# A chunked RWKV-7 recurrence inside a fused encoder trunk: triangular inverses from 8x8 blocks and four doubling levels in place of 4x4 blocks and five

## The chip, the cores and the metric

One core of one Trainium2 chip runs the whole program in one launch. The metric is the device time of one execution in microseconds. The kernel before takes 1693.85 us, the median of three runs (1692.18 to 1694.16).

## The reference, cut to what matters

The input is 256 tokens of 2048 channels, float32. Two layers follow each other. Each layer normalises x, multiplies it by one wide input matrix, and feeds three branches: a stick-breaking attention, a latent attention, and the RWKV-7 recurrence. The three gated results are projected, merged, projected once more and added to x. The change touches only the recurrence:

```python
def rwkv7_scan(r, decay, k, v, a_vec, b_vec):
    def step(state, inp):
        r_t, w_t, k_t, v_t, a_t, b_t = inp
        sa = jnp.einsum('bhij,bhj->bhi', state, a_t)
        state = (state * w_t[:, :, None, :] + sa[..., None] * b_t[:, :, None, :]
                 + v_t[..., None] * k_t[:, :, None, :])
        return state, jnp.einsum('bhij,bhj->bhi', state, r_t)
```

There are 8 heads of 64 channels. The kernel does not step through the tokens. It takes 128 tokens at a time, which turns the recurrence into matrix products and the inverse of one 128x128 unit triangular matrix for each head and each half of the sequence.

## The kernel before, in words

**The dense stream.** Most of the time goes to matrix products with weights read from memory. The weights come in chunks of two blocks of 128 rows by (mostly) 512 columns; there are 280 chunks in a layer. SyncE fetches a chunk into a ring of four slots. ScalarE copies it, rounded, into `w_hi` (the function `split` of the scalar program, line 1034), and VectorE subtracts to get the remainder `w_lo` (`split` of the vector program, line 1400). TensorE then runs 12 matmuls of 512 columns for the chunk (`dense_to`, line 730): two row blocks, two halves of the sequence, and three products of high and low parts. Before each chunk it waits for that chunk's `w_lo`. ScalarE and VectorE stay up to `LEAD` = 3 chunks ahead, and the four slots of `w_hi` and `w_lo` let them go no further.

**The order of the other work.** Everything else is cut into steps and laid between the chunks in an order written out by hand. `STEPS` (line 161) is a list of weights, one for each step; `beat_at` (line 165) spreads the steps over chunk positions 50 to 208 of each layer in proportion to the weights. Each engine's program calls `beat()` at the end of a step, and that issues its dense work up to the position. TensorE can stop at half a chunk; ScalarE and VectorE round the position down to a whole chunk. When VectorE's program has passed position n, it has issued the remainders of the chunks up to number n + 2 (counted from 0).

**The recurrence.** `rw_pair(p)` handles two heads, so it is run four times in a layer and eight times in all. The four matrices of a pair (two heads, two halves) are worked side by side. TensorE forms them (`rw_pe` count 2, lines 808 to 814), and VectorE copies them under a mask into `AM` (line 1529). Then:

- GpSimd gathers the 32x32 blocks on the diagonal of the four matrices into the compact tile `UC` (line 573).
- VectorE inverts the 4x4 blocks inside them. It picks three diagonals out of `UC` by a multiplication with a mask and a sum (lines 1539 and 1540), transposes them (1541), solves for the three diagonals of the inverse by six short operations (1544 to 1549), transposes back (1550), and spreads the diagonals over the columns again (1552 to 1554) into `WC`, `WT` and `WA`. One `beat()` lies between line 1550 and line 1552. These operations hang on each other, and `link` puts a semaphore wait on VectorE behind nearly every one. I call the part up to line 1550 the first part, and the rest the second part.
- Doubling levels follow on TensorE (line 816). A level is a group G1 of four small matmuls, a ScalarE copy of its result, a group G2 of four small matmuls, and an addition and transposes on VectorE. Levels 1 to 3 go from 4x4 to 32x32, level 4 to 64x64 and level 5 to 128x128.

The position of TensorE at which the pairs of a layer form their matrices is 50.5, 73.5, 92.5 and 111.5. From there it issues dense work for the next four steps and then begins level 1, at 55.5, 78.5, 97.5 and 116.5.

Of the kernel before, what the change touches and what calls it, by code (L numbers as in the profile page):

```python
# [32 lines left out]
ALU = mybir.AluOpType  # L33
ACT = mybir.ActivationFunctionType
X = mybir.AxisListType.X

DEPTH, SEQ, DM = 2, 256, 2048
P = 128
# [16 lines left out]
C_GATE = C_RG + RWW  # L55
DECAY = float(np.exp(-0.5))
MID = P // 2 - 1
LEVELS = 5
LEVELS_IN = 4
KC = 2  # L60
RING = 4
HALF_RING = 4
# [7 lines left out]


K_ID, K_INC, K_NTRI, K_NONE, K_RWM, K_LEV = 0, 128, 256, 384, 512, 1024
K_COS = K_LEV + 128 + 64 * LEVELS_IN
K_SIN = K_COS + 64
K_COL = K_SIN + 64
K_END = K_COL + 2
# [2 lines left out]
def constants():  # L79

    c = np.zeros((P, K_END), np.float32)
    i = np.arange(P)
    row, col = i[:, None], i[None, :]
    c[:, K_ID:K_ID + P] = row == col
    past_mid = (row <= MID).astype(np.float32)
    c[:, K_INC:K_INC + P] = -DECAY * ((row <= col).astype(np.float32) - past_mid)
    c[:, K_NTRI:K_NTRI + P] = -(row >= col).astype(np.float32)
    c[:, K_NONE:K_NONE + P] = -1.0
    strict, incl = (row < col), (row <= col)
    c[:, K_RWM:K_RWM + 512] = np.concatenate([strict, incl, strict, incl], 1)  # L90
    for q in range(4):
        r = slice(32 * q, 32 * q + 32)
        for k in range(4):
            at = K_LEV + 32 * k
            c[r, at:at + 32] = ((col == row + (k + 1) % 4) & (row // 4 == col // 4))[r, r]
        for n in range(LEVELS_IN):
            b = 2 ** (n + 1)
            joined = (row // (2 * b) == col // (2 * b)) & (row // b < col // b) | (n == 0)
            at = K_LEV + 128 + 64 * n + 32 * (q % 2)
            c[r, at:at + 32] = joined[r, r]  # L100
    half = ROPE // 2
    freqs = (np.float32(10000.0) ** (-np.arange(half, dtype=np.float32) / np.float32(half))).astype(np.float32)
    ang = np.arange(SEQ, dtype=np.float32)[:, None] * freqs[None, :]
    for h in range(HALVES):
        c[:, K_COS + h * half:K_COS + (h + 1) * half] = np.cos(ang[h * P:(h + 1) * P])
        c[:, K_SIN + h * half:K_SIN + (h + 1) * half] = np.sin(ang[h * P:(h + 1) * P])
    c[:, K_COL] = -DECAY * (i > MID)
    c[:, K_COL + 1] = -DECAY * (i <= MID)

    return c  # L110
# [39 lines left out]
AT_KK = AT_Z + 1  # L150
AT_DECAY = AT_KK + 9
AT_PAIRS = AT_DECAY + 5
RW_STEPS = [1, 1.2, 1, 1.5, 1.8] + [0.88, 0.98] * LEVELS + [0.85] * 6
LATENT_STEPS = [2, 2.5]
GN_STEPS = [0.9] * 8
ML_PREP, ML_VISITS = [1.1, 1.2, 1.3, 1.2, 1.4, 1.4], [2, 1.5, 1.4]
# [33 lines left out]
AT_RW, AT_ML1, AT_SB = END["mg1"] + 2, END["mg1"] + 4, END["br0"]  # L190


RW_PE, RW_ACT, RW_DVE, RW_POOL = 8 + 2 * LEVELS, 5 + LEVELS, 5 + 2 * LEVELS, 9


def program(nc, x, norm_g, w_in, mla_q_norm_g, mla_kv_norm_g, mla_w_uq, mla_w_ukv, mla_qn_g, mla_kn_g,
# [3 lines left out]
    with ExitStack() as ctx:  # L200
# [13 lines left out]
        con = sb("con", [P, K_END])  # L214
# [15 lines left out]
        def take(n):  # L230
            a = arena[:, used[0]:used[0] + n]
            used[0] += n
            assert used[0] <= ARENA, used[0]
            return a
# [4 lines left out]
        def units(n, u):  # L239
            return take(n).rearrange("p (u c) -> p u c", u=u)  # L240
# [10 lines left out]
        PV = halved(3072)  # L251
# [10 lines left out]
        UC, WC = units(128, 4), units(128, 4)  # L262
# [14 lines left out]
        WF = units(512, 4)  # L277
        WT, WT6, XB = units(256, 4), units(256, 4), units(256, 4)
        (WAE, WA), (LME, LM), (LM5E, LM5), (X5E, X5), (X6E, X6) = (edged() for _ in range(5))
        DIAG, DIAG_T, INVERSE = units(96, 3), units(96, 3), units(128, 4)  # L280
        ZEROS = arena[:, at_tb:used[0]]
        WIDE = take(512).rearrange("p (k u c) -> p k u c", k=4, u=4)
        QKM, PP = again(at_tb, lambda: units(1536, 12), lambda: units(768, 2))
        PT, = again(at_tt, lambda: units(768, 2))
        sb_tiles = [again(at_tb, *[lambda n=n: take(n) for n in (512, 384, 384)])]
# [37 lines left out]
        eps, eps_gn, bias_kk = cells(1), cells(1), cells(1)  # L323

        ident = con[:, K_ID:K_ID + P]
        diagonals = con[:, K_LEV:K_LEV + 128].rearrange("p (k c) -> p k c", k=4)
        level = [con[:, K_LEV + 128 + 64 * n:K_LEV + 192 + 64 * n] for n in range(LEVELS_IN)]
        ntri, none = con[:, K_NTRI:K_NTRI + P], con[:, K_NONE:K_NONE + P]
        cosx = con[:, K_COS:K_COS + 64].rearrange("p (h c) -> p h c", h=2)
        sinx = con[:, K_SIN:K_SIN + 64].rearrange("p (h c) -> p h c", h=2)  # L330
# [17 lines left out]
        preset = sem("preset")  # L348
# [157 lines left out]
        def _(pool):  # L506
# [7 lines left out]
            for l in range(DEPTH):  # L514
# [26 lines left out]
                nc.gpsimd.tensor_copy(AM[:, :, 0:P], ident.unsqueeze(1).to_broadcast([P, 4, P])).then_inc(preset[l], 1)  # L541
                nc.gpsimd.memset(ZEROS, 0.0).then_inc(preset[l], 1)
                pool.wait_ge(preset[l], 8)
                nc.gpsimd.memset(INVERSE[:, 3, :], 1.0).then_inc(preset[l], 1)
                gate, beats = [0], [0]

                def dense_to(end):
# [18 lines left out]
                for p in range(4):  # L566
# [4 lines left out]
                    for q in range(4):  # L571
                        r = slice(32 * q, 32 * q + 32)
# [4 lines left out]
                    for a in range(2):  # L577
                        r = slice(64 * a, 64 * a + 32)
# [8 lines left out]
                    if p < 3:  # L587
# [3 lines left out]
                        for d in range(4):  # L591
                            for i in range(4):
                                j = (i + d) % 4
# [25 lines left out]
                for p in range(4):  # L619
# [3 lines left out]
                    for d in range(4):  # L623
                        for i in range(4):
                            j = (i + d) % 4
# [46 lines left out]
                for n in range(12):  # L672
# [5 lines left out]
                    if 6 <= n < 10:  # L678
                        j = n - 6
# [3 lines left out]
                        c = slice(j * 512, (j + 1) * 512)  # L683
# [5 lines left out]
                    if n >= 5 and n % 3 == 2:  # L689
                        j = n // 3 - 1  # L690
# [696 lines left out]
        def _(dve):  # L1387
            v = nc.vector
            at, group, beats, order = [0], [GI["rg"]], [0], [0]

            def link(ins):

                order[0] += 1
                ins.then_inc(dve_seq, 1)
                dve.wait_ge(dve_seq, order[0])

            def tt(o, a, b, op):
                return v.tensor_tensor(o, a, b, op)  # L1398
# [117 lines left out]
            def rw_pair(p):  # L1516
                e = RW_PE * p
                c = slice(p * P, (p + 1) * P)
# [11 lines left out]
                last.then_inc(rw_dve, 1)  # L1530
                beat(2)
                dve.wait_ge(rw_pool, 4 * RW_POOL * l + RW_POOL * p + 4)
                def over_columns(t, n):
                    return t[:, 0:n, 0:4].unsqueeze(3).to_broadcast([P, n, 4, 32])

                def over_units(n):
                    return diagonals[:, 0:n, :].unsqueeze(2).to_broadcast([P, n, 4, 32])

                link(tt(WIDE[:, 0:3], UC.unsqueeze(1).to_broadcast([P, 3, 4, 32]), over_units(3), ALU.mult))
                link(v.tensor_reduce(DIAG[:, :, 0:4], WIDE[:, 0:3], axis=X, op=ALU.add))  # L1540
                link(v.transpose(DIAG_T, DIAG))
                d1, d2, d3 = (DIAG_T[:, k, :] for k in range(3))
                t1, t2 = WIDE[:, 3, 0, :], WIDE[:, 3, 1, :]
                tt(t1[:, 0:31], d1[:, 0:31], d1[:, 1:32], ALU.mult)
                link(tt(t2[:, 0:30], d2[:, 0:30], d1[:, 2:32], ALU.mult))
                tt(d2[:, 0:31], d2[:, 0:31], t1[:, 0:31], ALU.add)
                link(tt(d3[:, 0:30], d3[:, 0:30], t2[:, 0:30], ALU.add))
                link(tt(t1[:, 0:31], d1[:, 0:31], d2[:, 1:32], ALU.mult))
                link(tt(d3[:, 0:31], d3[:, 0:31], t1[:, 0:31], ALU.add))
                link(v.transpose(INVERSE[:, 0:3, :], DIAG_T))  # L1550
                beat()
                link(tt(WIDE, over_columns(INVERSE, 4), over_units(4), ALU.mult))
                link(tt(WIDE[:, 0:2], WIDE[:, 0:2], WIDE[:, 2:4], ALU.add))
                link(tt(WC, WIDE[:, 0], WIDE[:, 1], ALU.add))
                for g in range(2):
                    last = v.transpose(WT[64 * g:64 * g + 64, :, 32 * g:32 * g + 32], WC[64 * g:64 * g + 64, :, :])
                last.then_inc(rw_dve, 1)
# [4 lines left out]
                for n in range(1, LEVELS_IN):  # L1562
                    beat()
                    dve.wait_ge(rw_pe, 4 * RW_PE * l + e + 2 * n + 2)
                    for g in range(2):
                        half = slice(32 * g, 32 * g + 32)
                        t = WT[64 * g:64 * g + 64, :, half]
                        last = tt(t, t, G2[0:64, :, half], ALU.add)
                    last.then_inc(rw_dve, 1)
                    dve.wait_ge(rw_dve, 4 * RW_DVE * l + RW_DVE * p + 2 * n + 3)  # L1570
                    for q in (1, 3) if n == LEVELS_IN - 1 else range(4):
                        r = slice(32 * q, 32 * q + 32)
                        last = v.transpose(WA[r, :, q % 2 * 32:q % 2 * 32 + 32], WT[r, :, q // 2 * 32:q // 2 * 32 + 32])
                    last.then_inc(rw_dve, 1)
                    if p < 3:
                        if n == 1 and p:
                            dve.wait_ge(ops_moved, 3 * l + p)
                        for i in range(n - 1, n + (n == 3)):
                            s = (KK, R[:, :, 0:512], AA, R[:, :, 512:1024])[i]
                            last = v.transpose(OPS_TURN[:, :, i * P:(i + 1) * P], s[:, :, (p + 1) * P:(p + 2) * P])  # L1580
                        if n == 3:
                            last.then_inc(ops_turned, 1)
                    if n == LEVELS_IN - 1:
                        for q in range(4):
                            r = slice(32 * q, 32 * q + 32)
                            v.transpose(WF[r, :, r], WT[r, :, q // 2 * 32:q // 2 * 32 + 32])
                    beat()
# [156 lines left out]
            for l in range(DEPTH):  # L1744
# [26 lines left out]
                for i in range(3):  # L1771
# [3 lines left out]
                    c = slice(i * 512, (i + 1) * 512)  # L1775
# [113 lines left out]
                for j in range(4):  # L1889
                    dense_to(merged_at(j))  # L1890
                    for s in range(2):
                        dve.wait_ge(mt_act[l], 2 * j + s + 1)
                        k = slice(4 * j + 2 * s, 4 * j + 2 * s + 2)
# [31 lines left out]
```

## Time and profile before

| what | value |
|---|---|
| median of three runs | 1693.85 us |
| the profiled execution, first to last instruction (its span) | 1690.5 us |
| TensorE matmul busy | 1677.6 us (99%) |
| TensorE weight load busy | 1399.2 us (83%) |
| VectorE busy | 1134.9 us (67%) |
| ScalarE busy | 836.6 us (49%) |
| GpSimd busy | 487.8 us (29%) |
| bytes moved by DMA | 332.82 MB, mean 197 GB/s |
| granted TensorE clock | full speed in every slice |

The profiled execution has only its span as its own time; the timed runs also hold what lies ahead of the first and behind the last instruction, and their median is 3.35 us above that span. The page of the profile gives busy time by engine, the slices of the span, the chain of work that ended last, and the costliest groups of instructions. One caution applies to TensorE: matmuls overlap in its pipeline, so one that is listed with 0.39 us is followed by the next one 0.23 us after it began.

### The profile page before, as it was taken

To read this page: it belongs to the slowest core of one execution; us is meant where nothing else is said; L and a number is where in the kernel's file an instruction comes from. 1 tells how busy PE (TensorE), PEld (TensorE's weight loads), DVE (VectorE), ACT (ScalarE), POOL (GpSimd) and SP (SyncE) were. 2 spreads that over 40 slices of the span, in tenths; PEclk is the share of its full clock that TensorE was granted. 3 is DMA by queue.
4 is the path that set the end of the run, shared out by engine and by line. 5 is a ranking of instruction groups with operands and counts; after the bars stand their busy time and mean duration, and the time that the engine had idled before them with its cause. 6 is when DMAs were issued, how large, how long until landed. Compare 5 with 4: busy or idle time off the path is not lost.

```text
span 1690.5 us, 22088 instructions
## 1 busy us (share of the span) xinstructions
PE 1677.6 (99%) x8394; PEld 1399.2 (83%) x8394; DVE 1134.9 (67%) x1579; ACT 836.6 (49%) x1181; POOL 487.8 (29%) x722
## 2 busy tenths in 40 slices
PE   8999999999999999999999999999999999999999
PEld 7878888888888888888888788888888888888887
DVE  5668575766976566886656775756669666578853
ACT  6454453435544455554454454434445554555532
POOL 1011212410343426362410112233203534244500
PEclk9999999999999999999999999999999999999999
DMA  8865655655666557785687555556556565668754
GB/s 277 243 193 182 175 177 170 184 165 173 178 184 176 173 164 234 236 302 188 205 269 226 176 186 172 187 152 188 174 167 178 167 178 177 192 212 279 267 193 157
DMA packets 176913, 332.82 MB, mean 197 GB/s; under 512 B 19516, under 2 KB 32746, under 8 KB 176808
## 3 DMA queue, kind: packets, MB, share of 16 engines
q1 hardware_dynamic: 167048, 297.86, 57.7%
q0 software_dynamic: 9584, 33.48, 5.7%
q8 instruction: 66, 1.08, 0.3%
q14 instruction: 39, 0.32, 0.1%
q10 hardware_dynamic: 176, 0.07, 0.0%
HBM read 311.20 MB, written 16.78 MB: 194 GB/s over the span
## 4 chain that ended last, share of the span: by engine, by line
PE 92%; DVE 3%; ACT 2%; DMA 2%; issue 1%; SPq 1%; ACTq 0%; DVEq 0%
PE D L707 83%; PE B L707 8%; DMA ring<-in_w_in 2%; DVE w_lo L1398 1%; ACT w_hi L1026 1%; DVE xy L1398 0%; ACT arena L1026 0%; ACT gev L1026 0%; PE B L898 0%; DVE arena L1398 0%; DVE gev L1444 0%; PE B L877 0%; SPq L435 0%; ACT L1026 0%; DVE arena L1428 0%
## 5 line engine op out<-in xcount | busy, mean ns | idle before, releaser
L1398 DVE TENSOR_TENSOR w_lo<-ring,w_hi 128x1024 fp32r<-128x1024 f32 (+3 forms) x560 | 675.7, 1219 | 342.1 <-ACT w_hi L1026 334.0
L1026 ACT ACTIVATE w_hi<-ring 128x1024 fp32r<-128x1024 f32 (+3 forms) x560 | 575.0, 1038 | 463.9 <-PE D L707 361.5
L707 PE MATMUL D<-w_hi,ht_hi 128*128 128x512 f32 (+2 forms) x1728 | 681.3, 394 | 3.0 <-DVE w_lo L1398 2.8
L707 PE MATMUL D<-w_hi,ht_lo 128*128 128x512 f32 (+2 forms) x1728 | 666.0, 385 | 0.0
L707 PE MATMUL D<-w_lo,ht_hi 128*128 128x512 f32 (+2 forms) x1728 | 665.1, 385 | 0.0
L707 PEld LDWEIGHTS D<-w_hi,ht_hi 128*128 128x128 f32 x1728 | 325.1, 188 | 71.4 <-issue 7.8
L707 PEld LDWEIGHTS D<-w_hi,ht_lo 128*128 128x128 f32 x1728 | 324.5, 188 | 65.3
L707 PEld LDWEIGHTS D<-w_lo,ht_hi 128*128 128x128 f32 x1728 | 325.2, 188 | 59.0 <-issue 0.5
L609 POOL COPY arena<-arena 32x256 f32<-32x256 f32 x240 | 163.1, 680 | 144.7 <-DVE arena L1428 109.3
L707 PEld LDWEIGHTS B<-arena 128*66 128x66 f32 (+3 forms) x1312 | 134.2, 165 | 24.3 <-issue 8.2
L707 PE MATMUL B<-arena 128*66 128x64 f32 (+7 forms) x1312 | 144.7, 263 | 0.6 <-ACT arena L1026 0.6
L1026 ACT ACTIVATE arena<-B 64x128 f32<-64x128 f32 (+5 forms) x146 | 50.2, 350 | 189.2 <-PE B L707 183.9
L626 POOL COPY arena<-arena 32x384 f32<-32x384 f32 x128 | 95.7, 748 | 136.0 <-PE B L707 103.8
L707 PE MATMUL D<-w_hi,mt_lo 128*128 128x512 f32 x256 | 100.7, 393 | 0.0
L707 PE MATMUL D<-w_lo,mt_hi 128*128 128x512 f32 x256 | 100.4, 392 | 0.0
L707 PE MATMUL D<-w_hi,mt_hi 128*128 128x512 f32 x256 | 99.7, 389 | 0.0
L552 POOL DMA_DIRECT2D gate_spill<-gev x24 | 17.8, 742 | 246.9 <-ACT gev L1026 245.8
L1398 DVE TENSOR_TENSOR arena<-arena 128x1024 f32<-128x1024 f32 (+5 forms) x136 | 75.0, 561 | 5.1 <-DMA arena<-arena 1.6
L573 POOL COPY arena<-arena 32x128 f32<-32x128 f32 x32 | 24.4, 764 | 171.6 <-DVE arena L1529 170.2
L1026 ACT ACTIVATE arena<-arena 128x1024 f32<-128x1024 f32 (+5 forms) x88 | 59.0, 670 | 15.2 <-DVE arena L1398 11.6
L1026 ACT ACTIVATE gev<-D,small 128x512 f32<-128x512 f32 (+1 forms) x64 | 40.5, 681 | 45.0 <-PE D L707 44.8
L707 PEld LDWEIGHTS D<-w_lo,mt_hi 128*128 128x128 f32 x256 | 48.1, 188 | 11.0
(160 smaller groups left out, 1376.9 us busy)
## 6 DMA issues: line engine op xcount, KB each, us to landing
ring<-in_w_in SPq DMA_DIRECT2D x368, 512.0 KB, 4.5
ring<-in_w_out SPq DMA_DIRECT2D x64, 512.0 KB, 5.2
ring<-in_w_br_mla SPq DMA_DIRECT2D x32, 512.0 KB, 5.2
gate_spill<-gev POOLq DMA_DIRECT2D x24, 512.0 KB, 4.7
arena<-gate_spill POOLq DMA_DIRECT2D x24, 512.0 KB, 5.2
ring<-in_mla_w_ukv SPq DMA_DIRECT2D x16, 512.0 KB, 4.0
ring<-in_w_br_rw SPq DMA_DIRECT2D x16, 512.0 KB, 5.2
ring<-in_w_br_sb SPq DMA_DIRECT2D x16, 512.0 KB, 5.2
```

The lines of the kernel that those rows point to most:

```text
L552: pool.dma_start(spill[n].rearrange("(h p) c -> p h c", p=P), gev[:, n % 2, :, :]).then_inc(spilled[n % 2][l], 16)
L573: nc.gpsimd.tensor_copy(UC[r, :, :], AM[r, :, r]).then_inc(rw_pool, 1)
L609: nc.gpsimd.tensor_copy(moved[32 * j:32 * j + 32, :, :, i, :], turned[32 * i:32 * i + 32, :, :, j, :]).then_inc(quadrants[l], 1)
L626: nc.gpsimd.tensor_copy(moved[32 * j:32 * j + 32, :, i, :], turned[32 * i:32 * i + 32, :, j, :]).then_inc(ml_quarters, 1)
L707: return nc.tensor.matmul(o, a, b, start=start, stop=stop, skip_group_check=True)
L1026: return nc.scalar.activation(o, i, fn, **kw)
L1398: return v.tensor_tensor(o, a, b, op)
```

## The change

A block is now 8x8 (`EDGE`), so one doubling level goes: `LEVELS` 4 for 5, `LEVELS_IN` 3 for 4. VectorE picks seven diagonals instead of three. First it folds each row's own 8x8 block out of the 32 columns of `UC` into eight columns, `INNER`; the diagonals are taken from there. The seven diagonals of the inverse are solved by six rounds of two operations. The solution is spread over 8 columns (`SOLVED`) and then over 32. Scratch tiles move into `PV`, and the constants hold other masks. The weights of a pair's steps change, with the same sum of 20.9 as before. With them the same helper `beat_at` puts TensorE's level 1 at positions 57, 80, 99 and 117.5. GpSimd runs one level mask fewer. The operands of the next pair are turned two at a time in levels 1 and 2, not one, one and two in levels 1 to 3.

```diff
-LEVELS = 5
-LEVELS_IN = 4
+LEVELS = 4
+LEVELS_IN = 3
+EDGE = 8
...
-RW_STEPS = [1, 1.2, 1, 1.5, 1.8] + [0.88, 0.98] * LEVELS + [0.85] * 6
+RW_STEPS = [1, 1.2, 1, 1.7, 2.96] + [0.92, 1.02] * LEVELS + [0.88] * 6
...
-                link(tt(WIDE[:, 0:3], UC.unsqueeze(1).to_broadcast([P, 3, 4, 32]), over_units(3), ALU.mult))
-                link(v.tensor_reduce(DIAG[:, :, 0:4], WIDE[:, 0:3], axis=X, op=ALU.add))
+                blocks = own_block.unsqueeze(1).unsqueeze(3).to_broadcast([P, 4, 32 // EDGE, EDGE])
+                wide = WIDE[:, 0:128].rearrange("p (u j c) -> p u j c", u=4, j=32 // EDGE)
+                link(tt(wide, UC.rearrange("p u (j c) -> p u j c", c=EDGE), blocks, ALU.mult))
+                link(v.tensor_reduce(INNER, wide.rearrange("p u j c -> p u c j"), axis=X, op=ALU.add))
+                wide = WIDE[:, 0:32 * (EDGE - 1)].rearrange("p (k u c) -> p k u c", k=EDGE - 1, u=4)
+                link(tt(wide, INNER.unsqueeze(1).to_broadcast([P, EDGE - 1, 4, EDGE]),
+                        diagonals[:, 0:EDGE - 1, :].unsqueeze(2).to_broadcast([P, EDGE - 1, 4, EDGE]), ALU.mult))
+                link(v.tensor_reduce(DIAG[:, :, 0:4], wide, axis=X, op=ALU.add))
                 link(v.transpose(DIAG_T, DIAG))
-                d1, d2, d3 = (DIAG_T[:, k, :] for k in range(3))
-                t1, t2 = WIDE[:, 3, 0, :], WIDE[:, 3, 1, :]
-                tt(t1[:, 0:31], d1[:, 0:31], d1[:, 1:32], ALU.mult)
-                link(tt(t2[:, 0:30], d2[:, 0:30], d1[:, 2:32], ALU.mult))
-                tt(d2[:, 0:31], d2[:, 0:31], t1[:, 0:31], ALU.add)
-                link(tt(d3[:, 0:30], d3[:, 0:30], t2[:, 0:30], ALU.add))
-                link(tt(t1[:, 0:31], d1[:, 0:31], d2[:, 1:32], ALU.mult))
-                link(tt(d3[:, 0:31], d3[:, 0:31], t1[:, 0:31], ALU.add))
-                link(v.transpose(INVERSE[:, 0:3, :], DIAG_T))
+                link(v.tensor_copy(INVERSE_T, DIAG_T))
+                for m in range(1, EDGE - 1):
+                    n, c0 = EDGE - 1 - m, 32 - m
+                    link(tt(TERMS[:, 0:n, 0:c0], DIAG_T[:, 0:n, m:32],
+                            INVERSE_T[:, m - 1:m, 0:c0].to_broadcast([P, n, c0]), ALU.mult))
+                    solved = INVERSE_T[:, m:EDGE - 1, 0:c0]
+                    link(tt(solved, solved, TERMS[:, 0:n, 0:c0], ALU.add))
+                link(v.transpose(INVERSE[:, 0:EDGE - 1, :], INVERSE_T))
                 beat()
-                link(tt(WIDE, over_columns(INVERSE, 4), over_units(4), ALU.mult))
-                link(tt(WIDE[:, 0:2], WIDE[:, 0:2], WIDE[:, 2:4], ALU.add))
-                link(tt(WC, WIDE[:, 0], WIDE[:, 1], ALU.add))
+                wide = WIDE.rearrange("p (u c k) -> p u c k", u=4, c=EDGE)
+                link(tt(wide, INVERSE[:, :, 0:4].rearrange("p k u -> p u k").unsqueeze(2)
+                        .to_broadcast([P, 4, EDGE, EDGE]), diagonals.rearrange("p k c -> p c k").unsqueeze(1)
+                        .to_broadcast([P, 4, EDGE, EDGE]), ALU.mult))
+                link(v.tensor_reduce(SOLVED, wide, axis=X, op=ALU.add))
+                link(tt(WC.rearrange("p u (j c) -> p u j c", c=EDGE),
+                        SOLVED.unsqueeze(2).to_broadcast([P, 4, 32 // EDGE, EDGE]), blocks, ALU.mult))
...
-                        for i in range(n - 1, n + (n == 3)):
+                        for i in (2 * n - 2, 2 * n - 1):
```

## Rows read from the trace of the kernel before

**Rows 1.** The page: busy time by engine, and shares of the chain that ended last.
```profile
PE 1677.6 (99%) x8394; PEld 1399.2 (83%) x8394; DVE 1134.9 (67%) x1579; ACT 836.6 (49%) x1181; POOL 487.8 (29%) x722
PE 92%; DVE 3%; ACT 2%; DMA 2%; issue 1%; SPq 1%; ACTq 0%; DVEq 0%
```

**Rows 2.** Waits, whole span: waiter, releaser, us in total, times, longest.
```profile
PE D L707 <- DVE w_lo L1398: 2.8, 9, 0.5
```

**Rows 3.** Timeline of TensorE, third pair, layer 0: start, length, instruction.
```profile
293.16 0.50 PE L707 MATMUL D<-w_hi,ht_hi 128*128 128x512 f32 x1
...
297.19 0.39 PE L707 MATMUL D<-w_hi,ht_lo 128*128 128x512 f32 x1
...
299.91 0.39 PE L707 MATMUL D<-w_hi,ht_lo 128*128 128x512 f32 x1
...
305.57 0.39 PE L707 MATMUL D<-w_hi,ht_hi 128*128 128x512 f32 x1
...
306.94 0.64 PE L707 MATMUL B<-arena 128*66 128x64 f32 x8
...
310.24 0.64 PE L707 MATMUL B<-arena 128*66 128x64 f32 x8
```

**Rows 4.** Timeline of VectorE, GpSimd and ScalarE, same pair.
```profile
293.28 2.62 DVE L1529 COPY_PREDICATED arena<-con,B 128x512 f32<-128x512 uint32 x4 [3.25 <-PE B L707]
...
295.77 2.46 DVE L1398 TENSOR_TENSOR w_lo<-ring,w_hi 128x1024 fp32r<-128x1024 f32 x2
295.97 3.10 POOL L573 COPY arena<-arena 32x128 f32<-32x128 f32 x4 [18.72 <-DVE arena L1529]
...
299.11 0.56 DVE L1398 TENSOR_TENSOR arena<-arena,con 128x384 f32<-128x384 f32 x1 [0.88 <-POOL arena L573]
...
300.60 1.18 DVE L1398 TENSOR_TENSOR arena<-arena 128x31 f32<-128x31 f32 x6
...
302.12 2.36 DVE L1398 TENSOR_TENSOR w_lo<-ring,w_hi 128x1024 fp32r<-128x1024 f32 x2
303.06 1.27 ACT L1026 ACTIVATE gev<-D,small 128x512 f32<-128x512 f32 x2 [1.60 <-PE D L707]
...
307.61 0.56 ACT L1026 ACTIVATE arena<-B 64x128 f32<-64x128 f32 x2 [2.34 <-PE B L707]
```

**Rows 5.** Timeline of VectorE, first pair of layer 0.
```profile
152.33 2.64 DVE L1529 COPY_PREDICATED arena<-con,B 128x512 f32<-128x512 uint32 x4 [2.38 <-PE B L707]
...
158.41 0.56 DVE L1398 TENSOR_TENSOR arena<-arena,con 128x384 f32<-128x384 f32 x1 [1.22 <-POOL arena L573]
```

**Rows 6.** VectorE groups by line and shape: count, busy us, mean ns, idle before.
```profile
L1398 DVE TENSOR_TENSOR arena<-arena,con 128x128 f32<-128x128 f32 x48 | 12.0, 291 | 0.5
L1580 DVE STREAM_TRANSPOSE xy<-arena 128x256 f32<-128x256 f32 x18 | 7.3, 431 | 0.4
L1398 DVE TENSOR_TENSOR arena<-arena 128x31 f32<-128x31 f32 x32 | 6.2, 194 | 1.1
L1398 DVE TENSOR_TENSOR arena<-arena 128x256 f32<-128x256 f32 x14 | 6.0, 425 | 0.4
L1540 DVE TENSOR_REDUCE arena<-arena 128x12 f32<-128x384 f32 x8 | 4.4, 553 | 0.3
L1541 DVE STREAM_TRANSPOSE arena<-arena 128x96 f32<-128x96 f32 x8 | 2.2, 279 | 0.3
L1816 DVE COPY arena<-arena 128x128 f32<-128x128 f32 x2 | 0.5, 227 | 0.1
```

**Rows 7.** Timeline: TensorE waits for a `w_lo` that is late.
```profile
1296.58 1.21 DVE L1398 TENSOR_TENSOR w_lo<-ring,w_hi 128x1024 fp32r<-128x1024 f32 x1
...
1297.03 0.39 PE L707 MATMUL D<-w_hi,ht_lo 128*128 128x512 f32 x1
...
1297.85 0.50 PE L707 MATMUL D<-w_hi,ht_hi 128*128 128x512 f32 x1 [0.43 <-DVE w_lo L1398]
...
1298.18 0.40 PE L707 MATMUL D<-w_lo,ht_hi 128*128 128x512 f32 x1
```

More of the change, by code:

```diff
@@ L72 @@
 K_ID, K_INC, K_NTRI, K_NONE, K_RWM, K_LEV = 0, 128, 256, 384, 512, 1024
-K_COS = K_LEV + 128 + 64 * LEVELS_IN
+K_BLK = K_LEV + EDGE * EDGE
+K_JOIN = K_BLK + 32 // EDGE
+K_COS = K_JOIN + 64 * LEVELS_IN
 K_SIN = K_COS + 64
@@ L92, in constants @@
         r = slice(32 * q, 32 * q + 32)
-        for k in range(4):
-            at = K_LEV + 32 * k
-            c[r, at:at + 32] = ((col == row + (k + 1) % 4) & (row // 4 == col // 4))[r, r]
+        for k in range(EDGE):
+            at = K_LEV + EDGE * k
+            c[r, at:at + EDGE] = col[:, 0:EDGE] == row[r] % EDGE + (k + 1) % EDGE
+        c[r, K_BLK:K_BLK + 32 // EDGE] = row[r] % 32 // EDGE == col[:, 0:32 // EDGE]
         for n in range(LEVELS_IN):
-            b = 2 ** (n + 1)
+            b = EDGE // 2 * 2 ** n
             joined = (row // (2 * b) == col // (2 * b)) & (row // b < col // b) | (n == 0)
-            at = K_LEV + 128 + 64 * n + 32 * (q % 2)
+            at = K_JOIN + 64 * n + 32 * (q % 2)
             c[r, at:at + 32] = joined[r, r]
@@ L190 @@
 AT_RW, AT_ML1, AT_SB = END["mg1"] + 2, END["mg1"] + 4, END["br0"]
-RW_PE, RW_ACT, RW_DVE, RW_POOL = 8 + 2 * LEVELS, 5 + LEVELS, 5 + 2 * LEVELS, 9
+RW_PE, RW_ACT, RW_DVE, RW_POOL = 8 + 2 * LEVELS, 5 + LEVELS, 5 + 2 * LEVELS, 5 + LEVELS_IN
 def program(nc, x, norm_g, w_in, mla_q_norm_g, mla_kv_norm_g, mla_w_uq, mla_w_ukv, mla_qn_g, mla_kn_g,
@@ L279, in program @@
         (WAE, WA), (LME, LM), (LM5E, LM5), (X5E, X5), (X6E, X6) = (edged() for _ in range(5))
-        DIAG, DIAG_T, INVERSE = units(96, 3), units(96, 3), units(128, 4)
+        DIAG, INVERSE = units(32 * (EDGE - 1), EDGE - 1), units(32 * EDGE, EDGE)
         ZEROS = arena[:, at_tb:used[0]]
-        WIDE = take(512).rearrange("p (k u c) -> p k u c", k=4, u=4)
+        DIAG_T = units(32 * (EDGE - 1), EDGE - 1)
+        spare = [PV[:, 0, 256 * n:256 * n + 256] for n in range(4)]
+        WIDE = spare[0]
+        INVERSE_T = spare[1][:, 0:32 * (EDGE - 1)].rearrange("p (k c) -> p k c", k=EDGE - 1)
+        TERMS = spare[2].rearrange("p (k c) -> p k c", k=EDGE)
+        INNER, SOLVED = (spare[3][:, 32 * n:32 * n + 32].rearrange("p (u c) -> p u c", u=4) for n in range(2))
         QKM, PP = again(at_tb, lambda: units(1536, 12), lambda: units(768, 2))
@@ L325, in program @@
         ident = con[:, K_ID:K_ID + P]
-        diagonals = con[:, K_LEV:K_LEV + 128].rearrange("p (k c) -> p k c", k=4)
-        level = [con[:, K_LEV + 128 + 64 * n:K_LEV + 192 + 64 * n] for n in range(LEVELS_IN)]
+        diagonals = con[:, K_LEV:K_BLK].rearrange("p (k c) -> p k c", k=EDGE)
+        own_block = con[:, K_BLK:K_JOIN]
+        level = [con[:, K_JOIN + 64 * n:K_JOIN + 64 * n + 64] for n in range(LEVELS_IN)]
         ntri, none = con[:, K_NTRI:K_NTRI + P], con[:, K_NONE:K_NONE + P]
@@ L543, in _ @@
                 pool.wait_ge(preset[l], 8)
-                nc.gpsimd.memset(INVERSE[:, 3, :], 1.0).then_inc(preset[l], 1)
+                nc.gpsimd.memset(INVERSE[:, EDGE - 1, :], 1.0).then_inc(preset[l], 1)
                 gate, beats = [0], [0]
@@ L1532, in rw_pair @@
                 dve.wait_ge(rw_pool, 4 * RW_POOL * l + RW_POOL * p + 4)
[L1533 to L1537, printed above, removed]
-                link(tt(WIDE[:, 0:3], UC.unsqueeze(1).to_broadcast([P, 3, 4, 32]), over_units(3), ALU.mult))
-                link(v.tensor_reduce(DIAG[:, :, 0:4], WIDE[:, 0:3], axis=X, op=ALU.add))
@@ L1577, in rw_pair @@
                             dve.wait_ge(ops_moved, 3 * l + p)
-                        for i in range(n - 1, n + (n == 3)):
+                        for i in (2 * n - 2, 2 * n - 1):
                             s = (KK, R[:, :, 0:512], AA, R[:, :, 512:1024])[i]
                             last = v.transpose(OPS_TURN[:, :, i * P:(i + 1) * P], s[:, :, (p + 1) * P:(p + 2) * P])
-                        if n == 3:
+                        if n == LEVELS_IN - 1:
                             last.then_inc(ops_turned, 1)
```

## The prediction, made before the changed kernel was run

> **What bounds the kernel now.** I read the page first. TensorE is busy for 1677.6 of 1690.5 us, and 92% of the chain that ended last is TensorE's own work [rows 1]. Next I read the waits: TensorE stood waiting for a late `w_lo` for only 2.8 us in the whole span, in nine places [rows 2]. So an instruction taken from TensorE is worth its time, VectorE's time is worth nothing as long as the remainders come early enough, and a change that makes them late costs TensorE directly. Last I read the timelines of one pair of heads on TensorE [rows 3] and on the other engines [rows 4], because the change moves both of these.
>
> **What TensorE saves.** A level is two groups of four small matmuls. The two groups in rows 3 begin 3.30 us apart (306.94 to 310.24), and between them lie the first group and 12 dense matmuls. Twelve dense matmuls with nothing between take 2.72 us (297.19 to 299.91). So a group costs 0.58 us. Two groups in each of eight pairs are 16 groups, and 16 x 0.58 = 9.3 us saved. What goes with the level on VectorE (two additions, four transposes), ScalarE (two copies) and GpSimd (one mask) lies beside TensorE's work and brings nothing by itself.
>
> **What VectorE's first part takes now.** Before, it runs from 299.11 to 302.12, 3.0 us [rows 4]. The gap behind a linked operation is 0.03 us: from 300.60 to 302.12 lie 1.18 us of short operations and a transpose of 0.28 us [rows 4, 6], which leaves 0.06 us for two gaps. The new first part has 19 linked operations, priced along the rows of [rows 6] by elements per partition:
> - the multiplication with the block mask, 128 elements: 0.29 + 0.03 = 0.32 us;
> - the sum over it: the row for 384 elements is 0.55 us, the same as a multiplication of that size, so again 0.32 us;
> - the multiplication and the sum for seven diagonals, 224 elements, between 0.291 and 0.425 us: 0.39 + 0.03 = 0.42 us each;
> - two transposes of 224 elements, between 0.279 us (96) and 0.431 us (256): 0.43 us each with the gap;
> - the copy of 224 elements; the row for 128 elements is 0.227 us, and I take 0.30 us with the gap;
> - twelve operations in six rounds over 186, 150, 116, 84, 54 and 26 elements. Between 0.194 us (31), 0.291 us (128) and 0.425 us (256) these come to 0.352, 0.314, 0.279, 0.247, 0.217 and 0.189 us. With six gaps that is 1.78 us, and there are two operations in a round: 3.56 us.
>
> The sum is 0.64 + 0.84 + 0.86 + 0.30 + 3.56 = 6.20 us, against 3.0 us before.
>
> Its bounds: if short operations cost nearly nothing per element (0.19 us each for the twelve), the part takes 5.3 us. If rows of 26 to 31 elements, or reading every eighth element, run at half the rate per element, it takes 7.1 us (616 elements twice and 128 once, 1.05 ns each, with something off because not all is hit). Rows 6 show broadcasts at the full rate and no such stride, so I take 6.2.
>
> The Trainium skill's page "Vector Engine (DVE) Microarchitecture Reference", section "Measured stream behaviour on trn2", speaks against the change here: a port that steps over elements one by one loses up to about 1.5 ns on each. By it the sum into `INNER` (128 elements, stride eight) would take some 0.2 us more, and all eight pairs 1.5 us more. No row here shows such a stride.
>
> **What of it TensorE feels.** Before the first part VectorE issues the remainders up to position 52 in the first pair (94 in the third, and so on), which is two of them at 295.77 in [rows 4]. They cover TensorE to position 55.0 (97.0). TensorE restarts at 50.5 (92.5), so it meets the first missing `w_lo` after 4.5 chunks, 54 matmuls. In [rows 3] that is 293.16 to 305.57, 12.41 us. The new weights of the steps move level 1 back, but they do not put a remainder inside or ahead of the first part.
>
> The first part can begin only when GpSimd's four copies are done, 3.10 us in [rows 4]. It began 5.83 us after the masked copy in the third pair [rows 4] and 6.08 us after it in the first [rows 5]; the other six pairs lie between, and the mean of the eight is 5.95 us. The masked copy begins 0.12 us after TensorE's restart (293.28 to 293.16), so the part begins 6.07 us after the restart. Then come 6.20 us of first part and 1.21 us for the remainder behind it [rows 7]: 13.48 us. This is 1.07 us after TensorE wants it. In the kernel before the same sum is 6.07 + 3.0 + 1.2 = 10.3 us, 2.1 us early, and that reserve is what hides the part today.
>
> The handing over costs something too. In [rows 7] the late subtraction ends at 1297.79, the matmul begins at 1297.85, and the next one begins 0.33 us later instead of 0.23: 0.06 + 0.10 = 0.16 us. So TensorE loses 1.23 us in each pair, and eight pairs make 9.8 us.
>
> **What else moves.**
> - Second part, behind the remainder and one more: 256 elements twice, 128 once, two transposes and the mask of `WA` come to some 2.3 us, and then a third remainder. It ends 4.6 us after TensorE's late restart, and TensorE wants it after two chunks, 5.4 us. It is hidden with 0.8 us to spare. If both new operations ran at half rate (+0.5 us) it still would be.
> - G2 of level 1 stands half a chunk behind G1 in three of four pairs, where it was a whole chunk. ScalarE's copy between them takes 0.56 us and starts 0.67 us after G1, at 307.61 in [rows 4], 1.23 us against 1.9 us of TensorE's work. In the second pair G1 is at position 80, which is also the end of a gate group, and ScalarE's two evictions of it (1.27 us, as at 303.06 in rows 4) come ahead of the copy. That makes 2.2 us against 1.9: 0.3 us in each layer, 0.5 us with rounding. Bounds: nothing, and 1.3 us a layer.
> - The turned operands of the next pair come 0.4 of a step earlier, and GpSimd's 16 copies of them start no later than before. The lesser mask on GpSimd lies beside this. Both nothing.
> - VectorE has 1.1 us more in a pair (3.2 more in the first part, 0.3 less in the second, 1.8 less for the level). It idles a third of the span, so only the place matters, which is priced above.
>
> **The sum.** -9.3 + 9.8 + 0.5 = +1.0 us on the span of 1690.5 us. The runs shown have a median 3.35 us above the span, and nothing of the change touches that part. So 1693.85 + 1.0 = 1694.9 us. The measurement can tell about 0.2%, 3.4 us, from no change.
>
> **The rivals.**
> - *The first part stays hidden, and the saving is the result.* If the part takes 5.1 us or less (1.1 us under my sum), TensorE never waits and the time is 1693.85 - 9.3 + 0.5 = 1685 us. For it: the reserve of 2.1 us is real, and only a third of the extra 3.2 us has to go. Against it: the 19 operations would have to cost less than the flat price of 0.19 us for the twelve short ones. In between, every tenth of a microsecond off the part is worth 0.8 us. The result counts as faster when the part takes under 5.65 us.
> - *VectorE's part is longer than the sizes say (the other sign).* The place is the same remainder behind the first part; the mechanism is a slower rate of strided or short-rowed operands, or a wait by each of the 19 links that is longer than 0.03 us. At 6.8 us for the part, the wait is 1.83 us in each pair: 14.6 - 9.3 + 0.5 = +5.8 us, 1699.7 us. It decides from 6.5 us on, where the total passes +3.4 us. For it: all 19 operations hang on each other. Against it: the linked operations in the rows show only the 0.03 us.
> - *The remainders are late twice*, behind the second part too. It needs the second part to be 0.8 us longer than 2.3 us. Then some tenths of a microsecond are added in each pair, +1 to +4 us, at most 1699. I count it with the case before.
>
> **How the numbers follow.** The forecast case (the part between 5.65 and 6.5 us, a wait of 0.7 to 1.5 us in each pair) gets 0.46. The hidden or half hidden part, faster by over 0.2%, gets 0.22. The slower cases get 0.32. The range goes down to a part of 5.4 us (-6.4 from the forecast, 1688.5) and up to one of just under 7.0 us (+6.1, 1701.0). It leaves out the wholly hidden case and the worst lateness, together some 2 in 10.
>
> **What would show it.** Right: 64 fewer small matmuls (128 records fewer on TensorE); a row "PE D waits for DVE w_lo" of about 10 us, one wait of 1.1 to 1.3 us in each of eight pairs, each at the first chunk behind the first part; the first part 6.2 us long in the timeline of VectorE. Wrong: eight pairs without such a wait and a span of 1681 to 1682 us; a first part under 5.6 or over 6.6 us; TensorE waiting at the small groups of level 1 for `WT` or for ScalarE's copy more than for the remainders; or a wait at the chunk behind the second part.

## The result and the profile after

The changed kernel takes 1694.0 us, the median of 21 runs (1693.21 to 1695.92). The kernel before, run beside it, takes 1692.02 us in 21 runs. The ratio is 1.0012, with a 95% interval of 1.0007 to 1.0018. So the change makes the kernel slower by 2.0 us, clear of noise but within the 0.2% that the prediction called no change. The forecast was +1.0 us. The forecast of the time itself, 1694.9 us, lies closer than that, and this is luck: it was built on the median of three runs, 1693.85 us, which is 1.8 us above the median of 21. The span went from 1690.5 to 1692.1 us.

The page of the changed kernel, the rows that answer to [rows 1] and [rows 2] (engines, the chain, and the wait of TensorE for a late remainder: total, times, longest):

```profile
PE 1671.4 (99%) x8266; PEld 1392.0 (82%) x8266; DVE 1142.6 (68%) x1603; ACT 831.9 (49%) x1165; POOL 477.7 (28%) x714
...
PE 90%; DVE 6%; POOL 1%; DMA 1%; ACT 1%; issue 1%; SPq 0%; ACTq 0%; DVEq 0%
```

```profile
PE D L717 <- DVE w_lo L1408: 11.0, 12, 1.4
```

TensorE has 128 instructions fewer (8394 to 8266), which are the 64 small matmuls at two records each, and 6.2 us less work. In exchange it now waits 11.0 us for `w_lo`, not 2.8. The chain has 6% of VectorE in it where it had 3%, and 1% of GpSimd, which had none. These are the masked copy, GpSimd's gathering and the first part, which now lie ahead of the remainder for which TensorE waits.

Eight of those twelve waits are the pairs'. The timeline of TensorE in the changed kernel, only the instructions that waited, one for each pair:

```profile
166.48 0.50 PE L717 MATMUL D<-w_hi,ht_hi 128*128 128x512 f32 x1 [1.38 <-DVE w_lo L1408]
...
243.56 0.50 PE L717 MATMUL D<-w_hi,ht_hi 128*128 128x512 f32 x1 [1.04 <-DVE w_lo L1408]
...
372.79 0.50 PE L717 MATMUL D<-w_hi,ht_hi 128*128 128x512 f32 x1 [1.27 <-DVE w_lo L1408]
...
1004.09 0.50 PE L717 MATMUL D<-w_hi,ht_hi 128*128 128x512 f32 x1 [1.11 <-DVE w_lo L1408]
...
1081.17 0.50 PE L717 MATMUL D<-w_hi,ht_hi 128*128 128x512 f32 x1 [1.04 <-DVE w_lo L1408]
...
1145.77 0.50 PE L717 MATMUL D<-w_hi,ht_hi 128*128 128x512 f32 x1 [1.05 <-DVE w_lo L1408]
...
1210.46 0.50 PE L717 MATMUL D<-w_hi,ht_hi 128*128 128x512 f32 x1 [1.28 <-DVE w_lo L1408]
```

With the third pair (1.03, below) they add up to 9.20 us. The third pair of layer 0 in full, first TensorE (it answers to [rows 3]), from its restart to level 1:

```profile
294.53 0.50 PE L717 MATMUL D<-w_hi,ht_hi 128*128 128x512 f32 x1
...
306.72 0.39 PE L717 MATMUL D<-w_hi,ht_lo 128*128 128x512 f32 x1
308.14 0.50 PE L717 MATMUL D<-w_hi,ht_hi 128*128 128x512 f32 x1 [1.03 <-DVE w_lo L1408]
308.48 0.39 PE L717 MATMUL D<-w_lo,ht_hi 128*128 128x512 f32 x1
...
313.72 0.64 PE L717 MATMUL B<-arena 128*66 128x64 f32 x8
315.64 0.64 PE L717 MATMUL B<-arena 128*66 128x64 f32 x8
```

And VectorE in the same pair (it answers to [rows 4]). The part of lines 1546 to 1559 with the multiplications between them is the first part:

```profile
300.46 0.29 DVE L1408 TENSOR_TENSOR arena<-arena,con 128x128 f32<-128x128 f32 x1 [0.88 <-POOL arena L583]
300.78 0.39 DVE L1546 TENSOR_REDUCE arena<-arena 128x32 f32<-128x128 f32 x1
301.20 0.39 DVE L1408 TENSOR_TENSOR arena<-arena,con 128x224 f32<-128x224 f32 x1
301.63 0.39 DVE L1550 TENSOR_REDUCE arena<-arena 128x28 f32<-128x224 f32 x1
302.05 0.41 DVE L1551 STREAM_TRANSPOSE arena<-arena 128x224 f32<-128x224 f32 x1
302.50 0.28 DVE L1552 COPY arena<-arena 128x224 f32<-128x224 f32 x1
302.81 3.57 DVE L1408 TENSOR_TENSOR arena<-arena 128x186 f32<-128x186 f32 x12
306.42 0.41 DVE L1559 STREAM_TRANSPOSE arena<-arena 128x224 f32<-128x224 f32 x1
306.86 2.36 DVE L1408 TENSOR_TENSOR w_lo<-ring,w_hi 128x1024 fp32r<-128x1024 f32 x2
309.14 0.66 DVE L1408 TENSOR_TENSOR arena<-arena,con 128x256 f32<-128x256 f32 x1
...
311.28 0.43 DVE L1408 TENSOR_TENSOR arena<-arena,con 128x256 f32<-128x256 f32 x1
```

Read the two side by side. VectorE waits 0.88 us for GpSimd, begins the first part at 300.46 and ends it at 306.86, 6.40 us later. Only then does it begin the remainder that TensorE wants. TensorE issued its last matmul at 306.72, would have issued the next at 306.95, and issues it at 308.14.

From the restart to level 1 TensorE takes 19.19 us for 78 dense matmuls. In [rows 3] 60 matmuls took 13.78 us, and 18 more at 2.72 us a dozen are 4.08 us, together 17.86. So a pair loses 1.33 us, which is 0.3 us more than the idle time in the row. That column counts from the modelled end of the last matmul, and it does not hold the slow restart.

### The profile page after: what moved, and what is told of

Its sections match the earlier page's. It is cut to its first block, busy times and chain, and to the rows that moved or that the text cites. A ratio compares the mean times of both kernels' runs of the same rounds, so it can differ in the third digit from the quotient of the medians.

```text
span 1692.1 us, 21816 instructions
## 1 busy us (share of the span) xinstructions
PE 1671.4 (99%) x8266; PEld 1392.0 (82%) x8266; DVE 1142.6 (68%) x1603; ACT 831.9 (49%) x1165; POOL 477.7 (28%) x714
## 4 chain that ended last, share of the span: by engine, by line
PE 90%; DVE 6%; POOL 1%; DMA 1%; ACT 1%; issue 1%; SPq 0%; ACTq 0%; DVEq 0%
PE D L717 81%; PE B L717 8%; DVE arena L1408 2%; POOL arena L583 1%; DVE arena L1539 1%; DVE w_lo L1408 1%; DMA ring<-in_w_in 1%; ACT w_hi L1036 0%; DMA xy<-in_x 0%; PE B L908 0%; ACT arena L1036 0%; PE B L790 0%; PE B L887 0%; DVE arena L1559 0%; DVE arena L1551 0%
## 5 line engine op out<-in xcount | busy, mean ns | idle before, releaser
L717 PEld LDWEIGHTS B<-arena 128*66 128x66 f32 (+3 forms) x1184 | 124.2, 168 | 20.9 <-issue 7.7
L717 PE MATMUL B<-arena 128*66 128x64 f32 (+7 forms) x1184 | 134.4, 268 | 0.0
L1036 ACT ACTIVATE arena<-B 64x128 f32<-64x128 f32 (+5 forms) x130 | 45.7, 359 | 172.3 <-PE B L717 167.0
L1408 DVE TENSOR_TENSOR arena<-arena 128x1024 f32<-128x1024 f32 (+9 forms) x168 | 86.4, 515 | 5.1
L717 PEld LDWEIGHTS D<-w_hi,mt_lo 128*128 128x128 f32 x256 | 48.0, 188 | 11.2
```

The lines of the kernel that those rows point to most:

```text
L717: return nc.tensor.matmul(o, a, b, start=start, stop=stop, skip_group_check=True)
L1036: return nc.scalar.activation(o, i, fn, **kw)
```

## The experiments

Eight kernels were run. Ratios are to the kernel before in the same rounds: its median was 1691.67 us beside the first four kernels, 1692.18 beside the next three and 1692.36 beside the last.

### The remainder moved ahead of the first part

```diff
-RW_STEPS = [1, 1.2, 1, 1.7, 2.96] + ...
+RW_STEPS = [1, 1.2, 1.9, 1.5, 2.26] + ...
```

> The changed kernel with only the weights of a pair's steps altered (same sum): VectorE issues one more remainder before the first part, in the 0.9 to 1.2 us in which it stood idle for GpSimd's copies. TensorE's positions, its instructions and the first part stay as they are. Theory (a remainder comes late behind the first part because of its place, about 1.2 us in each pair): the eight waits go, TensorE's wait for w_lo falls from 11.0 us to about 2.5 us, and the time from 1694.0 to about 1684.5 us, ratio to the kernel before 0.995 to 0.996. Rival (VectorE's or the chain's total length is what costs, wherever it lies): the time stays near 1694 us, ratio 1.001. Rival (the waits only move to another place, level 1 or the next remainder): 1690 to 1694 us and waits of the same sum at another position.

Measured: 1684.35 us against 1691.67, ratio 0.9955 (0.9941 to 0.9969). VectorE's timeline in the third pair shows what moved. The single remainder at 298.16 is new there, and the first part begins behind it:

```profile
295.16 2.44 DVE L1408 TENSOR_TENSOR w_lo<-ring,w_hi 128x1024 fp32r<-128x1024 f32 x2
298.16 1.23 DVE L1408 TENSOR_TENSOR w_lo<-ring,w_hi 128x1024 fp32r<-128x1024 f32 x1 [0.56 <-ACT w_hi L1036]
299.57 0.29 DVE L1408 TENSOR_TENSOR arena<-arena,con 128x128 f32<-128x128 f32 x1 [0.19 <-POOL arena L583]
...
306.00 1.23 DVE L1408 TENSOR_TENSOR w_lo<-ring,w_hi 128x1024 fp32r<-128x1024 f32 x1
```

The new remainder lies where VectorE had stood idle for GpSimd, but it does not fit in there. VectorE first waits 0.56 us for ScalarE's copy and then 0.19 us for GpSimd, so it idles 0.75 us where it idled 0.88. The first part begins 7.02 us behind TensorE's restart at 292.55, and in the changed kernel it was 5.93 (294.53 to 300.46). GpSimd is held up too, its four copies in the changed kernel and in this one:

```profile
297.32 3.10 POOL L583 COPY arena<-arena 32x128 f32<-32x128 f32 x4 [18.26 <-DVE arena L1539]
```

```profile
295.34 4.20 POOL L583 COPY arena<-arena 32x128 f32<-32x128 f32 x4 [18.25 <-DVE arena L1539]
```

The gain comes from the order. The part begins 1.1 us later, but the first remainder behind it is wanted a whole chunk later, 2.72 us. It is ready at 307.23, and TensorE uses it at 307.68. All eight pairs' waits for `w_lo` are gone. The 4.2 us that are left, in six places, all lie ahead of the first pair of a layer. The first part is as long as before, so its place costs, not its length by itself. The first rival falls. Of the second, that the waits move elsewhere, 0.3 us is true: in the fourth pair of each layer, where level 1 stands six chunks behind the restart and not 6.5, TensorE now arrives before the transposes into `WT` are done:

```profile
372.52 0.69 PE L717 MATMUL B<-arena 128*66 128x64 f32 x8 [0.16 <-DVE arena L1569]
```

This version beats both kernels.

### The first part made longer

```diff
                 link(v.transpose(DIAG_T, DIAG))
+                for _ in range(3):
+                    link(v.transpose(DIAG_T, DIAG))
```

> The changed kernel with its first transpose (224 elements, 0.44 us with the gap) issued three more times in the first part, 1.3 us more there. Theory (no reserve is left, each microsecond of the first part is lost on TensorE in each pair): eight waits of about 2.5 us, 10.5 us more than the changed kernel, 1704.5 us, ratio 1.0075. Rival (the waits have another cause than the length of the first part): within 2 us of the changed kernel.

Measured: 1710.09 us, ratio 1.0109 (1.0096 to 1.0123): 16 us more than the changed kernel, not 10.5. The wait for `w_lo` rose as expected, from 11.0 to 22.4 us, with 2.38 to 2.73 us in each pair. Nearly all of the other 5 us is the granted clock, and the section on the hardware shows it. So the theory held for the wait, and the time missed for a reason that was not in it.

### The first part of the kernel before made longer by 1.2 us and by 3.4 us

```diff
                 link(v.transpose(DIAG_T, DIAG))
+                for _ in range(4):      # 11 in the second kernel
+                    link(v.transpose(DIAG_T, DIAG))
```

> The kernel before with its first transpose (96 elements, 0.31 us with the gap) issued four more times in the first part: 1.24 us more there, no level removed. Theory (a reserve of 2.1 us hides it): no wait is added, the ratio is 1.000 within its interval. Rival (VectorE's time costs in proportion): up to 10 us more, ratio 1.002 to 1.006.

> The kernel before with its first transpose issued eleven more times in the first part: 3.4 us more there, about what the 8x8 blocks add, and no level removed. Theory (3.4 less the reserve of 2.1 leaves 1.3 us late, and 0.16 for the handing over): eight waits of 1.3 to 1.4 us and 11 to 12 us more, 1703.5 us, ratio 1.007. Rival (the waits of the changed kernel come of its other step positions or of its strided operations): no more than 3 us slower, ratio under 1.002.

Measured: 1697.96 us with four, ratio 1.0038 (1.0024 to 1.0052), and 1716.88 us with eleven, ratio 1.0150 (1.0136 to 1.0164). Both are misses: 6 us where I expected none, and 25 where I expected 12. The waits of TensorE show why. With four more, the third pair, and with eleven more, the same pair:

```profile
309.42 0.69 PE L707 MATMUL B<-arena 128*66 128x64 f32 x8 [0.65 <-DVE arena L1558]
```

```profile
312.93 0.50 PE L707 MATMUL D<-w_hi,ht_hi 128*128 128x512 f32 x1 [1.01 <-DVE w_lo L1398]
...
316.11 0.69 PE L707 MATMUL B<-arena 128*66 128x64 f32 x8 [1.51 <-DVE arena L1558]
```

With four, no remainder of a pair is late, so the reserve at the remainders is more than 1.24 us. But the first group of level 1 waits for the transposes into `WT` (line 1558 there, 1556 in the kernel before). The kernel before, VectorE's second part in the third pair:

```profile
305.12 0.76 DVE L1398 TENSOR_TENSOR arena<-arena 128x256 f32<-128x256 f32 x2
305.91 0.63 DVE L1556 STREAM_TRANSPOSE arena<-arena 64x128 f32<-64x128 f32 x2
```

They end at 306.54, and the group begins at 306.94 [rows 3]. The reserve there is 0.4 us, and four transposes of 0.31 us overrun it by 0.84; from the restart to level 1 the third pair takes 14.58 us and not 13.78, 0.80 more. The kernel before has two reserves behind the first part, and the smaller one is at level 1. With eleven more both are overrun: waits of 10.7 us at the remainders and 12.2 us at level 1.

Two rivals are answered here. The time with four more, 1.0038, lies in the range of the rival that VectorE's time costs in proportion, and by itself could not reject it; the place of the waits does, and so does the run with the remainder moved ahead. With eleven more, the first part takes 6.38 us in the third pair of a kernel without the changed positions and operations, and the eight waits at the remainders are 1.00 to 1.35 us, where the changed kernel has 1.03 to 1.38 at 6.40 us. So these waits come from the length of the part, and not from the new positions of the steps or from strides as such.

### Three of the six rounds left out

```diff
-                for m in range(1, EDGE - 1):
+                for m in range(1, 4):
```

> The changed kernel with three of the six rounds of the solution (the diagonals four to seven are not completed, so the inverse is not the reference's). The first part is 1.5 us shorter, the places of the steps are the changed kernel's. Theory (length of the first part against a fixed place): it is 4.9 us instead of 6.4, the eight waits of 1.0 to 1.4 us go, and the time falls by 9 to 11 us to about 1684 us, ratio 0.995, the same as with the remainder moved ahead. Rival (every tenth of a microsecond of VectorE's time counts): the same sign, but then the run with the remainder moved ahead, whose VectorE does all the work, should not have reached 1684 us.

Measured: 1682.27 us, ratio 0.9942 (0.9928 to 0.9956). The wait for `w_lo` is 2.1 us in the whole span; none of the pairs waits. In the third pair the first part runs from 297.41 to 302.32:

```profile
297.41 0.29 DVE L1408 TENSOR_TENSOR arena<-arena,con 128x128 f32<-128x128 f32 x1 [0.88 <-POOL arena L583]
...
299.77 2.07 DVE L1408 TENSOR_TENSOR arena<-arena 128x186 f32<-128x186 f32 x6
301.88 0.41 DVE L1559 STREAM_TRANSPOSE arena<-arena 128x224 f32<-128x224 f32 x1
302.32 2.36 DVE L1408 TENSOR_TENSOR w_lo<-ring,w_hi 128x1024 fp32r<-128x1024 f32 x2
```

A shorter part in the old place and a full part in a better place give the same time within their intervals. This is the rival of the prediction in which the first part stays hidden, met on purpose: a part of 4.9 us, and no wait.

### Level 1 back at its old distance

```diff
-RW_STEPS = [1, 1.2, 1, 1.7, 2.96] + [0.92, 1.02] * LEVELS + [0.88] * 6
+RW_STEPS = [1, 1.2, 1, 1.5, 1.8] + [1.0, 1.1] * LEVELS + [1.0] * 6
```

> The changed kernel with the first five step weights of the kernel before, so that level 1 begins five chunks behind TensorE's restart as before, and not 6.5; the later steps are stretched to keep the sum of 20.9. Theory (there are two reserves: 2.1 us for the remainder, and only 0.3 us at level 1 for WT, of which the run with four more transposes showed the second): the eight waits for w_lo stay at 1.0 to 1.4 us, and eight waits of about 1.5 us at the first group of level 1 come on top, as with eleven more transposes; 13 us more than the changed kernel, about 1707 us, ratio 1.009. Rival (level 1's place does not matter as long as the remainders are the bottleneck): 1694 us.

Measured: 1707.79 us, ratio 1.0092 (1.0078 to 1.0105), as expected. Both kinds of wait, in total, times, longest:

```profile
PE D L717 <- DVE w_lo L1408: 12.5, 16, 1.4
PE B L717 <- DVE arena L1569: 12.1, 8, 1.5
```

Moving level 1 back by one to one and a half chunks is thus worth 14 us in the changed kernel. It opened the smaller reserve, and left the remainder's as it was.

### The TensorE work of one level put back by itself

```diff
-                beat(4)
+                beat(2)
+                pe.wait_ge(rw_dve, 4 * RW_DVE * l + d0 + 2)
+                for _ in range(2):
+                    for u in range(4):
+                        mm(B[3][0:66, 64 * u:64 * u + 64], con[:, 0:66], con[:, 0:64], u == 0, True)
+                    beat()
```

> The kernel with the remainder moved ahead, and with two groups of four matmuls (66 by 64, float32, their result unused) put back between the dense matmuls in each pair: TensorE's work of one level, alone, with nothing waiting for it. Theory (a group costs 0.58 us, 16 groups 9.3 us): 1684.4 + 9.3 = 1693.7 us, ratio to the kernel before 1.001. Rival (the level cost less than reckoned, and the gain of the moved remainder came from somewhere else): 1684 to 1690 us, ratio under 0.9985.

Measured: 1691.65 us, ratio 0.9995 (0.9986 to 1.0004). That is 7.3 us more than the kernel it was built on, where 9.3 was expected. From the two ratios the difference is 0.0040, and their intervals allow it to be between some 4 and 9.5 us. The trace is sharper on the groups. The two groups, with 12 dense matmuls between:

```profile
301.36 0.64 PE L717 MATMUL B<-con 128*66 128x64 f32 x8
...
304.64 0.64 PE L717 MATMUL B<-con 128*66 128x64 f32 x8
```

They begin 3.28 us apart, so a group costs 3.28 - 2.72 = 0.56 us, and sixteen cost 9.0 us. The two profiled executions differ by only 4.5 us (spans of 1684.7 and 1689.2). Of the missing 4.5 us, 2.9 lie outside the pairs, in the waits for late remainders (4.2 and 1.3 us), and 0.3 are the two waits at level 1, which are gone here. The rest, 1.3 us, is not explained.

### The remainder moved ahead in the kernel before

```diff
-RW_STEPS = [1, 1.2, 1, 1.5, 1.8] + ...
+RW_STEPS = [1, 1.2, 1.9, 0.8, 1.6] + ...
```

> The kernel before (4x4 blocks, five levels) with only the weights altered so that one more remainder is issued ahead of the first part, as in the run that reached 1684 us; no other position changes. Theory (the moved remainder is worth something only where a remainder is late, and here none is): 1692 us, ratio 0.9985 to 1.0015. Rival (the gain of that run came from the moved remainder itself and not from the level that went): about 7 us faster, ratio 0.996.

Measured: 1692.49 us against 1692.36, ratio 1.0002 (0.9993 to 1.0011). By itself the move is worth nothing. The 7 us of the first experiment are the level that went, most of it no longer paid back.

## Why the prediction was right, point by point

- **What a level is worth on TensorE.** 0.58 us a group, 9.3 us in all. The group by itself measured 0.56 us, 9.0 us in all. Right.
- **The length of the first part.** 6.20 us was the sum, 6.40 to 6.42 us the measurement. The twelve short operations took 3.61 us with the gap behind them (3.56 reckoned), the transposes 0.44 (0.43), the copy 0.31 (0.30). The sum into `INNER`, which reads every eighth element, took 0.39 us and not 0.29. That is half of the miss. The two sums over adjacent elements came out at the flat price (0.39 us for 224, and 0.42 us for 256 in the second part).
- **The stride.** The multiplication that reads `INVERSE` and the masks with strides took 0.66 us for 256 elements, where [rows 6] have 0.425. Both come to 0.8 to 0.9 ns for each strided element. No run changes the stride alone, so this stays a reading of two rows. The Trainium skill's page "Vector Engine (DVE) Microarchitecture Reference", section "Measured stream behaviour on trn2", says that a port which steps element by element loses time on each; the trace agrees, with less than the 1.5 ns that I drew from its row for steps of 24 words.
- **Where TensorE meets it.** At the first chunk behind the first part, once in each pair, was predicted, and it is so in all eight. The late part came to 1.19 us in the third pair (306.95 to 308.14), for 1.07 plus 0.06.
- **The handing over.** 0.16 us a pair was reckoned, 0.10 of it in the slow second matmul. That one begins 0.34 us after the first (308.14 to 308.48) and not 0.23. Right.
- **The loss in a pair.** 1.23 us predicted, 1.33 measured in the third. With 0.3 us on top of each idle row, the eight make 9.2 + 2.4 = 11.6 us, against 9.8. The first pair of layer 0 and the fourth pairs lose the most, 1.6 to 1.7 us, because their first part begins later behind the restart.
- **ScalarE's eviction in the second pair.** The groups G1 and G2 of level 1 there begin 2.04 us apart (249.14 and 251.18), and in the third 1.92. So 0.12 us a layer, for 0.3. Too large, and too small to matter.
- **The sum.** -9.0 + 11.6 + 0.2 = +2.8 us by the traces, +2.0 measured (1.2 to 3.0 by the interval), +1.6 from span to span, +1.0 predicted. The loss in the pairs, 1.8 us too small in all, is the term that was mis-sized, and most of that is the first part, 0.2 us too short in each of eight pairs. Two terms were not in the forecast and go the other way. TensorE's waits for remainders outside the pairs are 1.8 us and not 2.8, and two waits of 0.3 us for ScalarE's copy in the levels of the fourth pairs are gone. The first is no effect of the change as far as the runs show: in the kernels whose pairs do not wait for a remainder it is between 1.2 and 4.2 us.
- **What was wrong.** "That reserve is what hides the part today", of the 2.1 us at the remainders. It is not the one that counts in the kernel before: the reserve for `WT` at level 1 is 0.4 us. I had read both the end of the remainder and the start of the group, but not the end of the transposes against it. It did no harm to the forecast only because the change moves level 1 back, and that was luck. Had I asked which wait the new weights of the steps were to prevent, I would have found it. Two experiments on it missed, and the sixth then came out as expected from the corrected reading.
- **The rivals.** The hidden part would have needed under 5.1 us, and a part of 4.9 us was in fact hidden. The waits behind the second part did not come. The longer part came, at 6.4 us, just under the 6.5 from which that rival was to decide. So the forecast case, up to 6.5 us, held with little to spare.

So the expected gain of 9 us was there, and it was given back in the same pair, ahead of the levels, by a wait of the dense stream. The right answer to this change is not to undo it, but to issue one more remainder before the first part.

## What to carry to other kernels

When serial work on a helper engine grows, look for what is queued behind it in program order, not for the engine's idle share: here VectorE idled for a third of the span and still cost 11 us, because one 1.2 us subtraction stood behind the block. List every consumer behind the block with its own reserve, since the smallest decides, and moving one consumer back opens only that one. What can be done before the block's input is there is worth putting ahead of the block, even where it does not quite fit into the idle gap: the block began 1.1 us later here, and 1.2 us of waiting went in each pair.

## What the runs showed of the hardware that was not expected

A wait of about 2.4 us cost more than itself. In the kernel with three more transposes the granted clock fell behind three of the eight waits. The stretches around the third pair's wait, with the engines' busy time, the granted clock and the DMA share:

```profile
300.00:310.00 10.00, 10.00 (x46) 8.27 (x45) 8.59 (x20) 5.06 (x6) 4.93 (x8) 1.00 0.35 105
310.00:315.00 5.00, 2.59 (x10) 1.79 (x9) 4.72 (x11) 1.18 (x2) 0.22 (x1) 0.92 0.43 136
315.00:320.00 5.00, 5.00 (x18) 3.99 (x18) 4.83 (x8) 1.06 (x1) 0.00 (x0) 0.74 0.70 224
320.00:330.00 10.00, 10.00 (x68) 8.36 (x67) 5.50 (x13) 4.22 (x8) 0.73 (x1) 1.00 0.57 189
```

TensorE in the same stretch, one matmul after another:

```profile
312.99 0.50 PE L717 MATMUL D<-w_hi,ht_hi 128*128 128x512 f32 x1 [2.41 <-DVE w_lo L1408]
...
313.80 0.40 PE L717 MATMUL D<-w_hi,ht_hi 128*128 128x512 f32 x1
314.03 0.51 PE L717 MATMUL D<-w_lo,ht_hi 128*128 128x512 f32 x1
...
314.76 0.63 PE L717 MATMUL D<-w_hi,ht_hi 128*128 128x512 f32 x1
315.19 0.63 PE L717 MATMUL D<-w_lo,ht_hi 128*128 128x512 f32 x1
...
317.67 0.39 PE L717 MATMUL D<-w_lo,ht_hi 128*128 128x512 f32 x1
```

The matmuls first follow each other by 0.23 us, then from 314.3 to 317.3 by 0.43 us, the lower of the two clock levels (1.2 for 2.4 GHz), and then by 0.23 again. Seven matmuls lose 0.2 us each, 1.4 us in all, and the two at the edges lose a little. From the restart to level 1 this pair takes 22.15 us, and the second pair, whose wait of 2.38 us kept the clock, 20.55: 1.6 us. Three such places make 4.8 us, nearly all of the rest of that run's 16. The changed kernel's own waits of 1.0 to 1.4 us had no such stretch, and neither had the run with eleven more transposes, whose third pair waits 1.01 and 1.51 us three microseconds apart. The length of the wait alone does not decide: the clock fell behind waits of 2.41, 2.41 and 2.73 us, and it held behind five of 2.38 to 2.54 us. What does decide was not tried.

GpSimd's copies were slow beside VectorE's subtractions. The four copies of a pair have the same shape. In the third pair of the changed kernel the first two, which lie beside the two remainders, take 1.18 and 1.17 us, and the last two, while VectorE stands idle, 0.29 us each; that is the 3.10 us shown with the first experiment. With one more remainder there, the last copy takes 1.39 us, and it ends 0.16 us after the subtraction. In the first pair of layer 0 one copy takes 2.30 us, through both subtractions. So the start of the first part behind the masked copy, 5.83 to 6.08 us in the prediction, seems to be set in good part by VectorE's own remainders. It is not a fixed rule: in the kernel before with the remainder moved ahead, a copy that began 0.01 us ahead of the subtraction took 0.29 us, and the subtraction 1.36 instead of 1.22 us. No run was made to find the cause.
